# The output projection of a hybrid RWKV7 and latent-attention block, computed as seven block products

## The reference

```python
u = rms_norm(h, norm_mix); proj = u @ w_in          # 1024 x 4000 or so columns
y_a = rwkv7_branch(...)                             # recurrence over 8 heads, ends in @ w_o_rwkv
y_b = mla_branch(...)                               # causal attention, ends in @ w_o_mla
merged = sigmoid(gate_a) * y_a + sigmoid(gate_b) * y_b
h = h + merged @ w_out                              # 1024x1024 @ 1024x1024: the product that is changed
f = rms_norm(h, norm_ffn) @ w_ff_up
h = h + square(relu(f)) @ w_ff_down
return rms_norm(h, norm_final)
```

## Time and profile before

| | |
|---|---|
| median of three runs | 1504.9 us |
| profiled execution | 1505.54 us |
| its span | 1503.8 us |
| outside the span | 1.74 us |
| TensorE busy | 1470.0 us (98%) |
| TensorE's granted clock | full in every slice of the span |
| output projection on TensorE | 788.3 to 883.7 us, 384 matmuls 128x512 and 56 transposes |

### The profile page before, as it was taken

The page is one execution under the profiler, slowest core; times in us unless marked ns, Lnnn a source line. Parts: engine busy times, 40 slices in busy tenths (PEclk is TensorE's granted clock), DMA queues, the critical chain, the costliest instruction groups (busy, mean ns, idle before and its releaser), DMA issues.

```text
span 1503.8 us, 24849 instructions
## 1 busy us (share of the span) xinstructions
PE 1470.0 (98%) x9661; PEld 1212.4 (81%) x9661; DVE 1043.3 (69%) x1629; ACT 681.9 (45%) x1228; POOL 134.3 (9%) x164
## 2 busy tenths in 40 slices
PE   6999999999999999999999999999999999999998
PEld 5987888777777887887787888888888888888887
DVE  6476764578677672679755489777777757777785
ACT  7455664334433223666224246444444433333453
POOL 1024220000010010463000020000000000000000
PEclk9999999999999999999999999999999999999999
DMA  5031002723133436204446125444443699889754
GB/s 193 15 81 43 23 9 70 232 71 92 46 81 95 130 126 161 80 3 138 155 139 251 43 67 172 154 150 150 154 154 136 226 335 324 285 278 300 272 177 151
DMA packets 181115, 216.53 MB, mean 144 GB/s; under 512 B 28789, under 2 KB 115186, under 8 KB 180242
## 3 DMA queue, kind: packets, MB, share of 16 engines
q1 hardware_dynamic: 180942, 215.11, 43.6%
q10 hardware_dynamic: 68, 0.02, 0.0%
HBM read 156.20 MB, written 56.92 MB: 142 GB/s over the span
## 4 chain that ended last, share of the span: by engine, by line
PE 77%; DVE 12%; ACT 3%; DMA 3%; issue 2%; SPq 1%; POOL 0%; DVEq 0%; ACTq 0%; POOLq 0%
PE bank L3507 20%; PE bank L3571 14%; PE bank L3109 14%; PE bank L3413 4%; PE bank L3472 4%; PE bank L3007 3%; PE bank L3019 2%; PE bank L3034 2%; PE bank L2896 2%; DVE xprod L2304 2%; PE bank L2963 2%; PE bank L3044 2%; DVE xs L2306 1%; DVE hacc L2751 1%; DVE down_raw L2711 1%
## 5 line engine op out<-in xcount | busy, mean ns | idle before, releaser
L3109 PE MATMUL bank<-uT_hi,w_hi 128*128 128x512 f32 x432 | 170.8, 395 | 0.0
L3109 PE MATMUL bank<-uT_hi,w_lo 128*128 128x512 f32 x432 | 168.2, 389 | 0.0
L3109 PE MATMUL bank<-uT_lo,w_hi 128*128 128x512 f32 x432 | 168.2, 389 | 0.0
L3571 PE MATMUL bank<-mg_lo,mg_hi 128*128 128x512 f32 x576 | 134.8, 390 | 0.7 <-DVE mg_hi L2718 0.7
L3571 PEld LDWEIGHTS bank<-mg_lo,mg_hi 128*128 128x128 f32 x576 | 107.9, 188 | 24.2 <-DVE mg_hi L2718 1.9
L3571 PE MATMUL bank<-yh,mg_lo 128*128 128x512 f32 x384 | 118.2, 389 | 0.0
L1416 ACT ACTIVATE zbuf<-bank 128x512 f32<-128x512 f32 x54 | 32.2, 598 | 172.7 <-PE bank L3109 168.5
L1783 ACT ACTIVATE f<-f 128x512 f32<-128x512 f32 x64 | 40.5, 632 | 131.6 <-DVE f L2676 69.7
L3109 PEld LDWEIGHTS bank<-uT_hi,w_hi 128*128 128x128 f32 x432 | 81.1, 188 | 21.8 <-issue 5.2
L3109 PEld LDWEIGHTS bank<-uT_hi,w_lo 128*128 128x128 f32 x432 | 81.1, 188 | 17.4 <-issue 1.0
L3109 PEld LDWEIGHTS bank<-uT_lo,w_hi 128*128 128x128 f32 x432 | 81.1, 188 | 16.9
(11 more groups left out here) (513 smaller groups left out, 3744.4 us busy)
## 6 DMA issues: line engine op xcount, KB each, us to landing
down_raw<-in_w_ff_down SPq DMA_DIRECT2D x80, 512.0 KB, 4.7
down_raw<-f_spill SPq DMA_DIRECT2D x56, 512.0 KB, 4.7
f_spill<-x SPq DMA_DIRECT2D x80, 256.0 KB, 2.9
w_raw<-in_w_in SPq DMA_DIRECT2D x28, 512.0 KB, 4.3
sgate<-gate_spill SPq DMA_DIRECT2D x16, 512.0 KB, 4.3
up_a<-in_w_ff_up SPq DMA_DIRECT2D x16, 512.0 KB, 5.0
up_b<-in_w_ff_up SPq DMA_DIRECT2D x16, 512.0 KB, 4.1
f_spill<-f SPq DMA_DIRECT2D x32, 256.0 KB, 2.2
```

Of the source, the lines that this page charges most:

```text
L3109: ins = nc.tensor.matmul(ps[2 * slot + g][:], st[:, slot, k, :], mv[:, k, g * HALF:(g + 1) * HALF], start=(k == 0 and m == 0), stop=(k == ...
L3571: ins = nc.tensor.matmul(ps[4 * (q % 2) + t][:], st, mv_, start=(start and w == 0 and m == 0), stop=(stop and w == 1 and m == 2))
```

## The change

The 1024x1024 product becomes seven products of 512x512 blocks. `mg` is cut into four blocks of features and tokens, `w_out` into four blocks of rows and columns. B11, B21 and B22 are blocks of w_out; T1 to T4 are sums of its blocks. A11, A12, A22 are blocks of merged; S1 to S4 are sums of blocks. A product is 4 token tiles j x 4 k-tiles x 3 = 48 matmuls 128x512, so 336 in place of 384. Products that share an output block are added up in the same PSUM bank (start=False) or by another add_h; there are 28 add_h in place of 16.

The sums of w_out's blocks are made by POOL in the windows of the input projection (16 subtractions 128x1024, w = 4 to 11), from tiles that SP loads, and stored to DRAM (w_out_sums_spill). The raw merged values are kept in the space of mg; POOL makes S1, the difference block S2 and S4, and the lo halves of S1, S4 and A12. The lo halves of the transposed rows of tiles 0 to 3, and of the sums of tiles 4 to 6, are moved from DVE to POOL. At the hand-over to the up projection T5, T6 and T7 stand behind up products 0, 1 and 2.

```diff
+ADD_ORDER = [(kind, j) for kind in ("P1", "P7", "P4", "P6", "P5") for j in range(4)] + [(kind, j) for j in range(4) for kind in ("P2", "P3")]
+BLOCK_PRODUCTS = ("B11", "T3", "T4", "T2", "T1", "B21", "B22")
+LAST_ADD = 28
...
+                    if 4 <= w < 12:
+                        p = (w - 4) // 2
+                        if w % 2 == 0:
+                            sp.wait_ge(s_spo, 16)
+                            if p:
+                                sp.wait_ge(*s_tst(16 * p))
+                            for k in range(2):
+                                sp.dma_start(tb[:, 2 * k:2 * k + 2, :].rearrange("p b n -> p (b n)"),
+                                             a["w_out"][0][(4 * k + p) * P:(4 * k + p + 1) * P, :]).then_inc(s_tld.sem, 16)
+                        else:
+                            sp.wait_ge(*s_tsum(4 * p + 4))
+                            sp.dma_start(t_dram[:, p].rearrange("b p n -> p b n"), tb[:]).then_inc(s_tst.sem, 16)
...
-                for b in range(2):
-                    load_gates(b, b)
+                load_gates(0, 0)
+                sp.wait_ge(s_ge, 2 * RC)
+                load_gates(1, 1)
...
+                sp.wait_ge(s_yt, NT)
+                load_block(0)
...
+                sp.wait_ge(*s_tst(16 * 4))
+                load_block(1)
+                sp.wait_ge(s_po, 2 * KD)
+                load_block(2)
+                load_h(4, half0, s_hx)
+                load_block(3)
+                sp.wait_ge(s_mt, 2 * KD)
+                load_h(0, half1, s_hx01[0].sem)
+                load_block(4)
+                load_h(0, half0, s_hx01[1].sem)
+                load_block(5)
+                load_block(6)
+                load_h(4, half1, s_hx11.sem)
...
+                for p in range(4):
+                    pool.wait_ge(*s_tld(32 * (p + 1)))
+                    for n, (dst, x, y) in enumerate(((0, 1, 0), (1, 3, 1), (3, 3, 0), (2, 2, 3))):
+                        if n >= 2:
+                            pool.wait_ge(*s_tsum(4 * p + n))
+                        nc.gpsimd.tensor_tensor(tb[:, dst, :], tb[:, x, :], tb[:, y, :], ALU.subtract).then_inc(s_tsum.sem, 1)
...
                         spread_state(2 * i + 2)
+
+                pool.wait_ge(s_mt, 2 * (KD - 1))
+                for k in range(4):
+                    pool.wait_ge(s_mt, 2 * (k + 4) + 1)
+                    nc.gpsimd.tensor_tensor(s1_raw[:, k, :], a21_raw[:, k, :], a22_raw[:, k, :], ALU.add).then_inc(s_asum.sem, 1)
+                for k in range(4):
+                    pool.wait_ge(s_mgl, 2 * k + 2)
+                    nc.gpsimd.tensor_tensor(diff_raw[:, k, :], a22_raw[:, k, :], diff_raw[:, k, :], ALU.subtract).then_inc(s_asum.sem, 1)
+                pool.wait_ge(s_mt, 2 * KD)
+                pool.wait_ge(s_hm, 4)
+                for k in range(4):
+                    pool.wait_ge(*s_asum(4 + k + 1))
+                    nc.gpsimd.tensor_tensor(s4_raw[:, k, :], a12_raw[:, k, :], diff_raw[:, k, :], ALU.subtract).then_inc(s_asum.sem, 1)
+                for kind, hi_at in (("S1", 12), ("S4", 16), ("A12", 24)):
+                    hi, lo = a_split[kind]
+                    for k in range(4):
+                        pool.wait_ge(s_mgh, hi_at + k + 1)
+                        nc.gpsimd.tensor_tensor(lo[:, k, :], a_raw[kind][:, k, :], hi[:, k, :].bitcast(F32), ALU.subtract).then_inc(s_plo.sem, 1)
+
+                for i in range(4):
+                    sl = slice(i * P, (i + 1) * P)
+                    for w, raw in ((0, b11r), (1, b21r)):
...
+                    pool.wait_ge(*s_hTh(8 + 3 * j + 3))
+                    nc.gpsimd.tensor_tensor(t2[1][:, :, sl], t2r[:, :, sl], t2[0][:, :, sl].bitcast(F32), ALU.subtract).then_inc(s_plo.sem, 1)
 
                 for j in range(3):
...
+                merged_hi(0)
+                merged_hi(1)
+                round_block(0)
+                for n in range(2, KD):
+                    round_wo((n + 1) % 2, 16 * (n + 2), 2 * n) if n % 2 == 0 else round_wo((n + 1) % 2, 16 * (n + 3), 2 * n) if n < KD - 1 else None
+                    if n < 4:
+                        merged_hi(n)
+
+                round_block(1)
...
+                round_block(2)
+                round_sum("S1")
+                round_block(3)
+                round_sum("S4", 8)
+                act.wait_ge(s_hm, 8)
+                round_sum("S2")
+                round_block(4)
+                act.wait_ge(s_mgl, 16)
+                round_sum("A12")
+                round_block(5)
+                round_block(6)
...
                 for i in range(NT - 1):
+                    if i == 2:
+                        rows_high(0)
                     square_h(i)
                     root_h(i)
-                    if i:
+                    if i >= 2:
                         rows_high(i - 1)
-                round_up(0)
+                    if i == NT - 3:
+                        round_up(0)
                 round_up(1)
-                rows_high(NT - 2)
                 square_last()
                 root_h(NT - 1)
+                rows_high(NT - 2)
                 round_up(2)
...
+                merge_half(0, 0)
+                rest_wo(0, 3)
+                merge_half(0, 1, 3)
+                merged_low(0)
+                merge_half(1, 0, 3)
+                merge_half(1, 1)
+                merged_low(1)
+                low_block(0, range(2))
+                for n in range(2, KD):
+                    if n < KD - 1:
+                        rest_wo((n + 1) % 2, n + 2)
+                    if n == KD - 1:
+                        low_block(1, range(2))
+                    for g in range(2):
+                        merge_half(n, g)
+                    if n < 4:
+                        merged_low(n)
+                    if n == 2:
+                        low_block(0, range(2, 4))
+                low_block(1, range(2, 4))
+                low_sum("A22", 8)
+                low_block(2)
...
+                for n in range(4):
+                    add_h(n)
+                low_block(3)
+                for n in range(4, 8):
+                    add_h(n)
+                low_sum("S2", 20)
+                low_block(4)
+                for n in range(8, 12):
+                    add_h(n)
+                for n in range(12, 16):
+                    add_h(n)
+                    if n == 13:
+                        low_block(5)
+                low_block(6)
...
+                norm_h(5)
+                rows_sums(4)
+                rows_sums_low(4)
+                add_h(27)
                 rest_up(0)
+                norm_h(6)
+                rows_sums(5)
+                rows_sums_low(5)
                 rest_up(1)
-                rows_sums(NT - 2)
-                rows_sums_low(NT - 2)
-                add_h(2 * NT - 1)
-                norm_h(NT - 1)
+                norm_h(7)
+                rows_sums(6)
+                rows_sums_low(6)
                 rest_up(2)
...
+                def out_product(kind, q, j, bank, start):
+                    hi, lo = a_split[kind]
+                    bhi, blo = b_split[q % 3]
+                    tok = slice(j * P, (j + 1) * P)
+                    for k in range(4):
+                        for m, (st, mv_) in enumerate(((hi, bhi), (lo, bhi), (hi, blo))):
+                            ins = nc.tensor.matmul(ps[bank][:], st[:, k, tok], mv_[:, k, :], start=(start and k == 0 and m == 0),
+                                                   stop=(k == 3 and m == 2), skip_group_check=True)
...
+                pe.wait_ge(s_mgl, 8)
+                pe.wait_ge(s_wl, NW + 4)
+                pe.wait_ge(s_mt, 2 * (KD - 1))
+                for j in range(4):
+                    out_product("A11", 0, j, j, True)
+                pe.wait_ge(s_wl, NW + 8)
+                pe.wait_ge(s_mt, 2 * KD)
+                for j in range(4):
+                    out_product("S3", 1, j, 4 + j, True)
+                pe.wait_ge(s_mgl, 12)
+                pe.wait_ge(s_wl, NW + 12)
+                for j in range(4):
+                    pe.wait_ge(s_h, 5 + j)
+                    out_product("A22", 2, j, 4 + j, False)
+                pe.wait_ge(s_mgl, 16)
+                pe.wait_ge(s_wl, NW + 16)
+                for j in range(4):
+                    pe.wait_ge(s_h, 1 + j)
+                    out_product("S2", 3, j, j, False)
+                pe.wait_ge(*s_plo(4))
+                pe.wait_ge(s_wl, NW + 20)
+                for j in range(4):
+                    pe.wait_ge(s_h, 13 + j)
+                    out_product("S1", 4, j, j, False)
+                transpose_h(0)
+                pe.wait_ge(*s_plo(12))
+                pe.wait_ge(s_wl, NW + 28)
+                for j in range(4):
+                    if j >= 2:
+                        pe.wait_ge(s_h, 21 + 2 * (j - 2))
+                    out_product("A12", 5, j, 6 + j % 2, True)
+                    transpose_h(j + 1)
+                    pe.wait_ge(s_h, 17 + j)
```

(74 more changed lines are left out.)

274 lines of the change are left out of this document (114 added, 160 removed).

## The result

The changed kernel takes 1532.8 us (median of four, 1532.5 to 1533.2), the one before 1504.9: a ratio of 1.0183 (95% interval 1.0171 to 1.0195), 28 us slower. The forecast was 1514. The span is 1530.8 us, 27.0 longer.

A forecast was written before the change was run, and what follows sets the result against it. TensorE, busy 98%, was taken as the bound: -11.7 for work and waits gone, +1.6 merges, +10.6 hand-over, +8.7 POOL/DVE contention gave +9.2, 1514.7 profiled, median 1514; own range 1508 to 1521, 8 in 10 1500 to 1524.

The forecast's parts named there:

- 48 matmuls: Output projection: 48 matmuls 128x512 leave TensorE, transposes stay in number; -10.9 us.
- waits for nfb and wout: Output projection: TensorE's wait for tile 0's scaling behind nfb goes, as T0 moves behind five products; -0.8 us.
- weight sums, window 7: Input projection: POOL's weight sums block DVE in the window with least room, slack 1.8 us; +1.7, bounds 0 to 9.
- branch weights behind block 0: Merges: four ACT copies for block 0 ahead of the next wo_hi delay TensorE; +1.6 us, bounds +1 to +4.
- third product: Output projection, A22: DVE lows ahead of add_h(4) delayed by POOL beyond their slack; +2 us, bounds 0 to 13.
- hand-over: Start of up projection: products wait for weights' lows, some behind T5 to T7; +10.6 us, plus +5 for contention.
- rival 3: POOL and DVE take strict turns, 1.87 us per two-input DVE low; third product waits 13 us; 1527 us, chance 0.13.
- The slack of 7.6: Third product: without contention add_h(4) is done at about 802.8, product starts at 810.4, so 7.6 us spare.
- rival 1: DVE wins every turn or operations seldom meet: contention costs about 1 us, total 1505.5 us; chance 0.22.
- the +5 for POOL's turns: Hand-over: four links with a two-input SBUF DVE operation each wait one POOL operation of 1.28 us; bounds 0 to 6.

The follow-up runs named there:

- POOL later: Changed kernel with one wait added on POOL: its four S4 sums and the twelve lo halves behind them start only when the eighth add_h is done; 1527.3 us.

## Why the prediction was wrong

The sum of the trace against that of the prediction (us of span):

| term | forecast | measured | from |
|---|---|---|---|
| 48 matmuls | -10.9 | -10.9 | 0.228 from matmul to matmul, as before |
| waits for nfb and wout | -0.8 | -1.0 | 0.8 and 0.2, gone |
| weight sums, window 7 | +1.7 | +2.3 | row of window 10, 378.0 to 380.3 |
| branch weights behind block 0 | +1.6 | +1.2 | wait 1.5 to 2.7 |
| third product | +2 | +11.1 | wait at 826.8 |
| hand-over | +15.6 | +14.2 | 3.8 + 4.4 + 4.4 + 2.7, less 1.1 that this stretch lost before |
| slow clock | none | +10.5 | 1.6 + 1.6 + 3 x 1.84 + 1.8, in the profiled execution |
| sum | +9.2 | +27.4 | measured 27.0 |

**The step that failed** is the one that isn't in the sum: the prediction read "TensorE's clock is granted in full (2.4 GHz) in all of these stretches" and added up its waits, five of which were 2.5 to 5 us long, at their length alone. The level in the profile of before was one with no such wait in these stages; in the changed kernel's profile each wait that the forecast itself put in brought its own slow stretch. Priced at 1.7 each, the forecast would have been about +18 (9.2 + 5 x 1.7). The Trainium skill (TensorE: Matmul & The Clock Gate, Part 1) says that TensorE's default state is throttled and activity releases it; the trace agrees, with 0.43 us from matmul to matmul behind a wait of 2.7 us and 0.228 behind one of 1.3; in POOL later it is 0.228 behind one of 2.7 too.

**The second** is a size, the +2 at the third product, 11.1 measured. "POOL isn't at work all the time" failed: POOL was at work without a pause from 799.2 to 825.5, and rival 3's mechanism held, strict turns. The slack of 7.6 failed too: fourteen DVE lows and four adds stood ahead of add_h(4), not twelve lows, and they began at 801.0. At 0.60 each add_h(4) would have been done at about 812.5, 3.2 us ahead of TensorE (815.7). The fourteen took 22.6 us, 14.2 more than at 0.60, and 14.2 - 3.2 is the wait. These are estimates from the rows above. Rival 3's price per low (1.87) was near (1.71 in the full turns). That its 13 us are near 11.1 is in part luck: it counted twenty lows from 790 us on, eight of which stand behind add_h(4). The row at 685.74, which spoke for rival 1, is one meeting in which DVE's operation ran in full and POOL's two took 3.10; no row of before shows two full lists. The Trainium skill (SBUF — State Buffer, SBUF: two separate sides) says that whichever starts first gets the pair for the whole instruction and the other fully blocks. The trace agrees for one meeting (1.60 for DVE's low beside POOL's at 865 us, 0.69 alone); for two full lists it shows who starts next, the other one (1.71 for each).

What was right: the 10.9; the branch weights' wait and its cause; window 7 as the place where the weight sums cost; and the hand-over without its clock, wait by wait (3.9, 4.7, 4.7 and 2.7 forecast, with the +5 for POOL's turns spread evenly; 3.8, 4.4, 4.4 and 2.7 measured), with products 1 and 2 behind T5 and T6: DVE stood still for 3.0 us until T5's banks came. What it didn't say is that only part of these waits can be had back by order: with the up weights moved ahead, product 4's rose from 2.7 to 7.8.

The change bought 10.9 us of TensorE with 12 more adds and 16 + 12 sums, and moved lows to POOL so that DVE should bear it. But where both have two-input SBUF operations of 128x512, one on POOL keeps DVE waiting for 1.1 us (1.71 - 0.60), and on DVE it would take 0.6.

## What to carry to other kernels

Ahead of moving two-input SBUF work from DVE to POOL, look at whether DVE has such work of its own in the same microseconds: if so, POOL's operation can cost DVE more than doing it would. Here that held in mid-projection and not at the hand-over, and moving all of it back gave 3.1 us. To a wait of TensorE of 2.2 us or more in a dense stage add 1.7 us of slow clock as an estimate, and know that it was 0 to 3.1; waits of up to 1.5 us cost only their length here. Where TensorE is 98% busy and the stage behind it is handed over through DVE, count DVE's operations between the last product and the first that needs them all, before counting matmuls saved.

## What the runs showed of the hardware that was not expected

- Turns: two full lists of two-input 128x512 operations go at 1.71 us a pair, DVE 0.60 and the rest POOL's; DVE's operations with an input in PSUM go at 0.60 in between.
- Clock, in the same stretches of the sixteen profiles: behind waits of 1.0 to 1.5 us it stayed at 2.4 GHz in 17 of 17 cases. Behind waits of 2.2 to 11.1 us it was at 1.2 GHz for a while in 57 of 62, at a cost of 1.4 to 3.1 us. The same wait of 11.1 cost 1.5 in the changed kernel and 3.1 with the up weights ahead; one of 2.7 cost 1.6 there and nothing in POOL later.
- Executions of kernels with such waits scatter more: 1508.5 to 1516.3 in one whose profile has three, where the kernel before has 1503.7 to 1508.6 beside it. That the varying clock price makes this scatter is likely and not shown.
